# Two dense weight slots of a branch moved between the attention steps of the last two heads, and a convolution started during head 4

## The reference, cut to what matters

```python
proj = u @ w_in
a1, a2 = split(a_in);            a = a1 * sigmoid(a2)                 # branch A
a = causal_depthwise_conv(a, conv_a_w) + conv_a_b                     # 31 taps, 512 channels
y_a = (silu(layer_norm(a)) * silu(a_gate)) @ w_a_out
xb, gb, gc = split(b_in)                                              # branch B
yb = gb * causal_depthwise_conv(gc * xb, conv_b_w)                    # 3 taps
y_b = (yb * silu(b_gate)) @ w_b_out
o = causal_block_attention(qf, kf, v)                                 # branch C, 8 heads
y_c = (o * silu(c_gate)) @ w_c_out
m = sigmoid(g_a) * y_a + sigmoid(g_b) * y_b + sigmoid(g_c) * y_c
x = layer_norm(alpha * x + gate * (m @ w_o))
```

## Time and profile before

| quantity | value |
|---|---|
| median of 3 timed runs | 1769.42 us (1767.83 to 1771.9) |
| the profiled execution | 1767.57 us |
| its span in the trace | 1765.6 us |
| mean granted TensorE clock | 0.987 |
| PE busy, DVE busy, ACT busy | 97%, 60%, 39% of the span |

### The profile page before, as it was taken

How to read it: one execution, slowest core, us unless ns; L and a number is a source line. 1 busy time by engine, 2 the same in 40 slices (tenths; PEclk the granted TensorE clock), 3 DMA queues, 4 the chain that set the end, 5 groups by cost and what they waited for, 6 DMA issues and landing times.

```text
span 1765.6 us, 20420 instructions
## 1 busy us (share of the span) xinstructions
PE 1712.9 (97%) x8190; PEld 1385.5 (78%) x8190; DVE 1067.1 (60%) x1729; ACT 691.9 (39%) x1055; POOL 120.7 (7%) x114
## 2 busy tenths in 40 slices
PE   8999999999999999999899999999999899999996
PEld 8776666888888887878688888887878688888885
DVE  7445555866665446744478766668644368866565
ACT  4435563422222234465522232532555532333532
POOL 2100000011100000100000000012200000100012
PEclk9999999999999999999999999999999999999998
DMA  4411003455554221221122222221322122222221
GB/s 173 149 72 49 25 24 108 147 202 197 196 197 171 108 95 71 96 86 58 48 95 96 96 96 95 96 96 48 119 96 72 48 72 96 95 96 96 96 96 48
DMA packets 29533, 177.40 MB, mean 100 GB/s; under 512 B 3614, under 2 KB 3758, under 8 KB 12287
## 3 DMA queue, kind: packets, MB, share of 16 engines
q1 hardware_dynamic: 20448, 144.71, 22.6%
q0 software_dynamic: 8608, 31.21, 5.1%
q10 hardware_dynamic: 382, 0.19, 0.0%
HBM read 171.28 MB, written 4.78 MB: 100 GB/s over the span
## 4 chain that ended last, share of the span: by engine, by line
PE 77%; DVE 4%; issue 1%; ACT 1%; DVEq 0%; ACTq 0%
PE ps L612 24%; PE ps L614 24%; PE ps L613 24%; PE ps L1129 1%; PE ps L1111 1%; DVE h L1661 1%; PE ps L1117 1%; DVE ps L2073 1%; ACT w_hi L1209 1%; PE ps L650 0%; ACT Pc L1209 0%; PE ps L1198 0%; DVE cacc L1668 0%; DVE w_lo L1661 0%; PE ps L1181 0%
## 5 line engine op out<-in xcount | busy, mean ns | idle before, releaser
L612 PE MATMUL ps<-Xh,w_hi 128*128 128x512 f32 (+1 forms) x1664 | 652.9, 392 | 5.2 <-DVE Xl L1661 3.4
L614 PE MATMUL ps<-Xh,w_lo 128*128 128x512 f32 (+1 forms) x1664 | 638.6, 384 | 0.0
L613 PE MATMUL ps<-Xl,w_hi 128*128 128x512 f32 (+1 forms) x1664 | 638.4, 384 | 0.0
L1661 DVE TENSOR_TENSOR w_lo<-w_raw,w_hi 128x2048 fp32r<-128x2048 f32 (+1 forms) x158 | 311.6, 1974 | 247.5 <-ACT w_hi L1209 247.3
L1209 ACT ACTIVATE w_hi<-w_raw 128x2048 fp32r<-128x2048 f32 (+1 forms) x152 | 259.4, 1709 | 297.4 <-DMA w_raw<-in_w 276.0
L612 PEld LDWEIGHTS ps<-Xh,w_hi 128*128 128x128 f32 x1664 | 312.9, 188 | 77.8 <-issue 16.0
L613 PEld LDWEIGHTS ps<-Xl,w_hi 128*128 128x128 f32 x1664 | 313.0, 188 | 64.6 <-issue 5.5
L614 PEld LDWEIGHTS ps<-Xh,w_lo 128*128 128x128 f32 x1664 | 312.6, 188 | 62.2
L1668 DVE SCALAR_TENSOR_TENSOR cacc<-ain,vec,cacc 128x512 f32<-128x512 f32 x240 | 162.9, 749 | 0.0
L1209 ACT ACTIVATE gt<-ps 128x512 f32<-128x512 f32 x48 | 28.6, 596 | 194.3 <-PE ps L614 194.3
L1209 ACT ACT_TABLE_LOAD x54 | 69.3, 1283 | 4.0 <-issue 3.0
(11 more groups left out here) (306 smaller groups left out, 2101.0 us busy)
## 6 DMA issues: line engine op xcount, KB each, us to landing
w_raw<-in_w SPq DMA_DIRECT2D x134, 1024.0 KB, 4.8
ada_w<-in_w_ada POOLq DMA_DIRECT2D x48, 512.0 KB, 4.6
bias_scratch<-brow POOLq DMA_DIRECT2D x2, 1312.0 KB, 5.8
h<-in_xT SPq DMA_DIRECT2D x4, 512.0 KB, 5.8
out<-h SPq DMA_DIRECT2D x4, 512.0 KB, 2.6
bias<-bias_scratch POOLq DMA_DIRECT2D x1, 1024.0 KB, 8.6
bias<-bias_scratch POOLq DMA_DIRECT2D x1, 512.0 KB, 4.7
cact<-in_c POOLq DMA_DIRECT2D x1, 512.0 KB, 6.7
```

What stands on the lines that cost most here:

```text
L612: nc.tensor.matmul(o_, whi, xhi, start=start, stop=False)
L613: nc.tensor.matmul(o_, whi, xlo, start=False, stop=False)
L614: return nc.tensor.matmul(o_, wlo, xhi, start=False, stop=stop)
L1661: return nc.vector.tensor_tensor(o_, a_, b_, op)
```

## The change

Heads 6 and 7 now take the first two slots of branch B between their steps, as heads 0 to 5 take branch A's. On PE `half_slot` has no bound, and the loop over branch B starts at its third slot. On ACT and DVE the slot splits go on for all eight heads; ACT reads the first tile of these two slots into `sig` with a Copy; DVE multiplies it with the second tile into `bx`. `conv_taps` is called in heads 4 and 5 (6 taps each) and in heads 6 and 7 (5 each), then 9 taps in each of branch B's third and fourth slots and 5 in each of the last four. In SBUF, `cacc` (the convolution's sum) now lies over the queries of heads 0 to 3, `bx` behind it, and the gate tiles `gt` over `bx`.

```diff
-        bx = sb("bx", [P, KC, CB - 1 + T], offset=R0)
-        o_cacc = at[0]
-        cacc = sb("cacc", [P, KC, T])
+        cacc = sb("cacc", [P, KC, T], offset=R0)
+        o_bx = at[0]
+        bx = sb("bx", [P, KC, CB - 1 + T])
...
-        gt = sb("gt", [P, 4, T], offset=R0)
-        assert at[0] <= o_cacc
+        gt = sb("gt", [P, 4, T], offset=o_bx)
+        assert at[0] <= o_yb
...
                 def half_slot(i, j):
-                    if i < 6:
-                        if j == 0:
-                            split_ready(G + (L_A + i))
-                        pair_tile(G + (L_A + i), j, fills).then_inc(tile_full if j == 0 else slot_done, 1)
+                    if j == 0:
+                        split_ready(G + (L_A + i))
+                    pair_tile(G + (L_A + i), j, fills).then_inc(tile_full if j == 0 else slot_done, 1)
...
-                for s in range(L_B, L_M):
+                for s in range(L_A + HEADS, L_M):
                     pair_slot(G + s, fills)
...
                 def a_tile(i, j):
-                    if i >= 6:
-                        return
-                    if i >= 4:
+                    if 4 <= i < 6:
...
-                        act_(sig, bank(0), ACT.Sigmoid).then_inc(bank_read[0], 1)
+                        act_(sig, bank(0), ACT.Sigmoid if i < 4 else ACT.Copy).then_inc(bank_read[0], 1)
 
                 for hd in range(HEADS):
-                    if hd < 6:
-                        next_hi(L_A + hd + 1)
+                    next_hi(L_A + hd + 1)
...
-                for s in range(8):
+                for s in range(2, 8):
                     next_hi(L_B + s + 1)
...
                 for hd in range(HEADS):
-                    if hd < 6:
-                        next_lo(L_A + hd + 1)
+                    next_lo(L_A + hd + 1)
...
                     elif hd < 6:
+                        if hd == 4:
+                            ve.wait_ge(bank_read[1], bf.f[1].val())
                         tf.add(1)
                         bf.take(0)
                         bf.take(1)
+                        conv_taps(6)
+                    else:
+                        s = hd - 6
+                        tf.add(1)
+                        conv_taps(5)
+                        bf.take(1)
+                        ve.wait_ge(bank_read[0], bf.take(0))
+                        ve.wait_ge(slot_done, G + (L_B + s + 1))
+                        nc.vector.memset(bx[:, s, 0:CB - 1], 0.0)
+                        tt(bx[:, s, CB - 1:CB - 1 + T], sig, bank(1), ALU.mult).then_inc(bank_read[1], 1)
                 gate_c(3)
...
-                nc.vector.memset(bx[:, :, 0:CB - 1], 0.0)
-                for s in range(8):
+                nc.vector.memset(bx[:, 2:4, 0:CB - 1], 0.0)
+                for s in range(2, 8):
...
-                    conv_taps(8 if s < 4 else 6)
+                    conv_taps(9 if s < 4 else 5)
```

More of the change, by code:

```diff
@@ L2086, in gate_c @@
                           split0 + (KD + 5 + i), KD + 5 + i)
-                for hd in range(HEADS):
-                    if hd < 6:
-                        next_lo(L_A + hd + 1)
[L2091 to L2108, removed]
                 taps = [(t0 + e, k) for t0 in range(0, KC, 2) for k in range(TAPS) for e in range(2)]
@@ L2127, in conv_taps @@
                     del taps[:n]
-                nc.vector.memset(bx[:, :, 0:CB - 1], 0.0)
-                for s in range(8):
+                for hd in range(HEADS):
+                    next_lo(L_A + hd + 1)
+                    max2(hd, 0)
+                    for b in range(NB):
+                        if b + 1 < NB:
+                            max2(hd, b + 1)
+                        norm2(hd, b)
+                    if hd and hd % 2 == 0:
+                        gate_c(hd // 2 - 1)
+                    if hd < 4:
+                        tf.add(1)
+                        ve.wait_ge(slot_done, G + (L_A + hd + 1))
+                        bf.take(1)
+                        ve.wait_ge(bank_read[0], bf.take(0))
+                        tt(ain[:, hd, TAPS - 1:TAPS - 1 + T], sig, bank(1), ALU.mult).then_inc(bank_read[1], 1)
+                    elif hd < 6:
+                        if hd == 4:
+                            ve.wait_ge(bank_read[1], bf.f[1].val())
+                        tf.add(1)
+                        bf.take(0)
+                        bf.take(1)
+                        conv_taps(6)
+                    else:
+                        s = hd - 6
+                        tf.add(1)
+                        conv_taps(5)
+                        bf.take(1)
+                        ve.wait_ge(bank_read[0], bf.take(0))
+                        ve.wait_ge(slot_done, G + (L_B + s + 1))
+                        nc.vector.memset(bx[:, s, 0:CB - 1], 0.0)
+                        tt(bx[:, s, CB - 1:CB - 1 + T], sig, bank(1), ALU.mult).then_inc(bank_read[1], 1)
+                gate_c(3)
+                nc.vector.memset(bx[:, 2:4, 0:CB - 1], 0.0)
+                for s in range(2, 8):
                     next_lo(L_B + s + 1)
```

## The result

The changed kernel takes 1760.02 us (median of 4 runs, 1756.48 to 1760.86) against 1769.70 before (4 runs): a ratio of 0.9945, 95% interval 0.993 to 0.996. On another chip it was 1759.17 against 1769.13, ratio 0.994 (0.9928 to 0.9953). So it is 9.7 to 10.0 us faster. 12.6 were forecast; 1760.0 lies inside the range (1752 to 1764) and 3.1 us above the forecast.

What follows compares the result with a forecast made beforehand. PE, busy 97% of the span, bounds the kernel, so only its waits pay. Slots save 17.15 us, head 5's delay costs 4.58: 12.57 us off 1769.42 gives 1756.9 us (chance 0.60), range 1752 to 1764.

Steps and rivals of the forecast that it cites:

- The slots' gain: Heads 6 and 7, given a slot each, take 30.95 us like heads 2 and 3; 17.15 us saved over both layers.
- The delay of head 5: Head 4's six taps on DVE make head 5's maxima and last transposes 2.29 us later a layer, 4.58 together.
- rival (a): The clock falls in head 5, costing 1.7 to 3.4 us a layer: 1760.4 to 1763.7 us; chance 0.13.
- head 5's hole: PE's wait among head 5's transposes: 1.75 us already before the change, expected 2.29 us longer with it.
- the argument against it: Head 5's 5.0 us of only transposes is half the shorter stretch before earlier clock falls, with dense work right around it.
- the clock leaves 1.00 in heads 5 to 7: Sign that the forecast is wrong; it expected the granted clock at 1.00 there.
- rival (b): Heads 6 and 7 get holes too, 1.75 us a head and layer, up to 7.0: 1763.9 us; chance 0.11.
- The taps' duration: Head 4's six taps on DVE take 3.56 us, 0.663 apart; the drain's some 0.45 us more a tap was left out.
- The four fewer taps later: Four fewer taps in the merge stage, 60 before it against 56, counted as nothing, perhaps 0.2 us either way.

Runs made afterwards that it cites:

- the taps in head 5: Changed kernel with head 4's six taps moved behind head 5's last division (12 there, none in head 4): 1749.91 us against 1769.13 before, ratio 0.9889.
- the hole filled: Changed kernel with dummy matmuls between head 5's transposes, where PE waits: 1754.85 us against the changed kernel's 1759.17.
- the taps ahead of the wait: Changed kernel with head 4's six taps between the product of `gate_c` and its remainder: 1750.75 us against 1769.13 before, ratio 0.9894.
- the taps alone: Kernel before with the new SBUF places and 6 taps each in heads 4 and 5, heads 6 and 7 without slots: 1775.54 us against 1767.47, ratio 1.0043.
- twelve taps: Changed kernel with all twelve taps in head 4 and none in head 5: 1769.94 us in one run, against 1767.89.
- the slots alone: Changed kernel with no tap in the attention loop, 7 in branch B's last four slots, 11 and 9 in gate slots: 1754.06 us against 1767.47 before, ratio 0.9919.

## Why the prediction was right, and where it was 3 us off

- **The slots' gain, 17.15 us: right in the traces.** Measured in four profiles (the changed kernel, the taps in head 5, the hole filled, the taps ahead of the wait) by 30.95 or so for heads 6 and 7, and as a whole by a span 17.4 us shorter once the taps are out of the way. Reading the cost of a covered pair of heads off heads 2 and 3 was enough. By medians it is 19.2, and not all of that is explained. The sum took what the clock costs in the bare heads from one execution; the bare heads of the taps alone lost 0.9 us more.
- **The delay of head 5, 2.29 us a layer: right to the hundredth**, in its place and its size, and shown by moving, doubling and shrinking the taps.
- **The clock, rival (a): this is the term that was mis-sized.** The sum carried nothing for it and gave it 0.13. It took 1.6 us in the first layer and 1.1 in the second of the first profile and 1.6 and 2.4 in the other (22.27, 21.80, 22.29 and 23.10 less 20.67), against the rival's 1.7 to 3.4 a layer. The rival's time began at 1760.4; 1760.0 was measured. The clock fell in every layer of every run in which head 5's hole was this long or longer: four times in the changed kernel, twice each with the taps alone and with twelve taps, and never where the hole was 1.75 us or was filled.
- **Why the argument against it failed.** It compared the hole's 5.0 us with 10.7 and 13.6 us counted from head 6's scores. But in the bare heads head 7's scores stand in between, and PE is busy throughout them; only behind them come ten transposes with waits, the same work as in head 5's hole. The two starts in the kernel before, and the clock around the first fall:

```profile
863.08 2.32 PE L1111 MATMUL ps<-K,Q 128*128 128x128 f32 x8
870.00:871.00 1.00, 0.31 (x5) 0.08 (x4) 0.00 (x0) 0.60 (x1) 0.00 (x0) 0.87 0.00 0
...
1401.63 2.33 PE L1111 MATMUL ps<-K,Q 128*128 128x128 f32 x8
```

  The first fall is at 871.00 - 2 x 0.13 = 870.74, 5.3 us after these scores end at 865.40; the second at 1406.64, 2.7 us after their end at 1403.96. In the changed kernel's first profile the falls are at 854.5 and 1387.0, 5.3 and 3.5 us after the last dense matmul, which ends at 849.17 and 1383.50. The stretches are alike in length too: 5.5 us from head 7's scores to the value products at 870.94, 4.9 us from 849.17 to the second dense tile at 854.05. So the rows before already showed two falls out of two behind a stretch like the new one. The Trainium skill, TensorE: Matmul & The Clock Gate, section What's actually happening, has half speed as the default and activity as what lifts it; by that rule the hole was at risk, and here the trace agrees with it.
- **What was luck.** The prediction names as a sign of being wrong that the clock leaves 1.00 in heads 5 to 7. It did, in both layers of both profiles: what happened is rival (a) and not the forecast. The time is inside the range because the range was drawn to take in (a) and (b). With the 1.6 and 1.1 us of the first profile the sum becomes 12.57 - 2.7 = 9.9 us, against 9.7 measured: that fits. With the 1.6 and 2.4 of the other it becomes 12.57 - 4.05 = 8.5, against 10.0 measured; that difference stays open, beyond the 0.9 us above.
- **Heads 6 and 7 hidden, rival (b): right.** In head 7's part of DVE's list the five taps had 0.21 us to spare before the product; the forecast had this place at 0.2 and a further 0.8 us behind it, and the ten transposes are again one group of 1.25 us.
- **The taps' duration and the Trainium skill's drain** (VectorE: DVE Perf Modes, The DRAIN you can't avoid): six taps behind head 5's last division took 4.06 us, as in the earlier trace rows; by the prediction's estimate of 0.45 us more a tap they would take about 6.8, so leaving it out was right. The same section says that a next instruction that is not held starts earlier, which the prediction did not take in and with which the trace agrees: the taps start 0.663 us apart, where the last one of five is shown as 3.40 - 4 x 0.663 = 0.75 us long.
- **The four fewer taps later, counted as nothing:** no run tests these four. PE waits for no weight split behind the attention loop in the trace before or in the one after; it does so with 14 fewer taps before the merge stage (the slots alone, 0.68 us a layer).

## What to carry to other kernels

When work is put into an engine's idle time, look at which instruction ends that idle time and put the work in front of it: the same 3.56 us cost nothing ahead of the wait and 2.3 us and more behind it. Where a change leaves the matrix engine with a hole of short transposes and waits, as the 5 us here, put a price on the granted clock behind it too, and try dummy matmuls in the hole. To judge such a hole by one that the trace already has, count that one from the last matmul that kept the engine busy, not from the start of the whole slow part. And when a changed kernel is faster, still try its parts one by one: here six taps in one place were costing 9 of the 19 us that the rest of the edit brought.

## What the runs showed of the hardware that was not expected

A kernel with ten more dummy matmuls on the busiest engine, five in each layer, was 4.3 us faster than the same kernel without them. The clock stayed at 2.4 GHz over the filled hole and fell to 1.2 GHz behind the unfilled one, in which PE was still busy for about 40% of the time with transposes (0.33, 0.44 and 0.40 of the three whole microseconds from 850 to 853). The same place cost different amounts in different executions: of one kernel's second layer, 3.4 us at half speed in one profile and 6.9 in the other.
